# Key pages and probabilities turned by VectorE in 32x32 blocks, values four pages at a time, weight splits on GpSimd

## What is computed

```
h = rmsnorm(x);  q,k,v,g_a,u,v_s,g_b,m_a,m_b = split(h @ w_in)        # 1024 x 5632
prompt:  causal attention over its own 512 keys (8 heads of 64), bias by distance
sample b: 16 cache pages of 128 tokens (table page_table[b]); blocks of 256 tokens
   gate  = q . mean(k of block);  keep the 3 best of 8 blocks per head and query
   s     = q . k + bias;  softmax over the kept pages and the new tokens;  out = p @ v
y_a = attn * silu(g_a);   y_b = gelu(u) * (tril(w_s) @ layernorm(gelu(v_s)) + b_s) * silu(g_b)
y   = rmsnorm(x + (sigmoid(m_a) * (y_a @ w_pa) + sigmoid(m_b) * (y_b @ w_pb)) @ w_o)
```

## Time and profile before

| | us |
|---|---|
| median of three runs | 585.2 |
| the profiled execution, its own time | 585.09 |
| its span, first to last instruction | 583.3 |

### The profile page before, as it was taken

The page is one execution under the profiler, slowest core; times in us unless marked ns, Lnnn a source line. Parts: engine busy times, 40 slices in busy tenths (PEclk is TensorE's granted clock), DMA queues, the critical chain, the costliest instruction groups (busy, mean ns, idle before and its releaser), DMA issues.

```text
span 583.3 us, 14963 instructions
## 1 busy us (share of the span) xinstructions
PE 571.0 (98%) x6072; PEld 524.7 (90%) x6072; DVE 315.3 (54%) x749; ACT 211.9 (36%) x461; POOL 24.3 (4%) x39
## 2 busy tenths in 40 slices
PE   8999999999999999999999999999999999999994
PEld 6999999998899899999889998999999999998763
DVE  5622324345456555666756666786463255695514
ACT  5523222334333434543454451241153241234313
POOL 2101111000000000000000000010000000000002
PEclk9999999999999999999999999999999999999998
DMA  8447334755586766767576577885879857152003
GB/s 263 133 164 236 112 111 129 213 187 179 168 256 182 235 189 206 223 195 243 173 234 210 183 253 248 281 251 169 259 236 338 286 179 257 57 190 88 1 8 145
DMA packets 73421, 111.89 MB, mean 192 GB/s; under 512 B 5485, under 2 KB 35194, under 8 KB 73354
## 3 DMA queue, kind: packets, MB, share of 16 engines
q1 hardware_dynamic: 71978, 107.33, 57.5%
q0 software_dynamic: 1232, 3.36, 2.0%
q10 hardware_dynamic: 144, 0.26, 0.1%
HBM read 106.39 MB, written 4.53 MB: 190 GB/s over the span
## 4 chain that ended last, share of the span: by engine, by line
PE 95%; DVE 2%; issue 1%; ACT 1%; POOL 0%; POOLq 0%; DVEq 0%; ACTq 0%
PE BK L497 43%; PE BK L643 9%; PE BK L517 8%; PE BK L848 7%; PE BK L655 6%; PE BK L669 5%; PE BK L579 2%; PE BK L720 2%; PE BK L727 2%; PE BK L531 2%; PE BK L737 2%; PE BK L773 1%; PE BK L695 1%; PE BK L868 1%; PE BK L564 1%
## 5 line engine op out<-in xcount | busy, mean ns | idle before, releaser
L497 PE MATMUL BK<-XH,WH 128*128 128x272 f32 x672 | 212.4, 316 | 0.0
L497 PE MATMUL BK<-XH,WL 128*128 128x272 f32 x672 | 194.3, 289 | 0.0
L497 PE MATMUL BK<-XL,WH 128*128 128x272 f32 x672 | 193.2, 288 | 0.0
L497 PEld LDWEIGHTS BK<-XH,WH 128*128 128x128 f32 x672 | 126.7, 189 | 9.9 <-issue 8.7
L497 PEld LDWEIGHTS BK<-XL,WH 128*128 128x128 f32 x672 | 127.2, 189 | 0.0
L497 PEld LDWEIGHTS BK<-XH,WL 128*128 128x128 f32 x672 | 126.5, 188 | 0.0
L1141 DVE TENSOR_TENSOR WL<-WRAW,WH 128x1024 fp32r<-128x1024 f32 x51 | 62.2, 1220 | 37.5 <-ACT WH L897 37.3
L643 PE MATMUL BK<-CST,KRAW 128*128 128x128 f32 x512 | 77.2, 273 | 0.8 <-DVE ATS L1330 0.5
L643 PEld LDWEIGHTS BK<-CST,KRAW 128*128 128x128 f32 x512 | 60.7, 141 | 2.5 <-issue 2.3
L1239 DVE COPY KT<-BK 128x512 f32<-128x512 f32 x64 | 44.0, 687 | 32.8 <-PE BK L643 32.7
L897 ACT ACTIVATE WH<-WRAW 128x1024 fp32r<-128x1024 f32 x52 | 54.8, 1055 | 18.6 <-PE BK L517 18.6
(11 more groups left out here) (205 smaller groups left out, 803.4 us busy)
## 6 DMA issues: line engine op xcount, KB each, us to landing
KRAW<-in_cache_k SPq DMA_DIRECT2D x128, 256.0 KB, 3.5
VRAW<-in_cache_v SPq DMA_DIRECT2D x120, 256.0 KB, 3.8
WRAW<-in_w_in SPq DMA_DIRECT2D x21, 1024.0 KB, 6.0
WO<-in_w_o SPq DMA_DIRECT2D x4, 1024.0 KB, 7.8
XR<-in_x_prompt SPq DMA_DIRECT2D x4, 512.0 KB, 5.6
VEX<-in_cache_v SPq DMA_DIRECT2D x8, 256.0 KB, 4.9
WRAW<-in_w_pb SPq DMA_DIRECT2D x4, 512.0 KB, 6.4
WRAW<-in_w_pa SPq DMA_DIRECT2D x4, 512.0 KB, 5.9
```

What stands on the lines that cost most here:

```text
L497: last = mm(BK[h][:, 0:HALF], w[:, n % 2, k, :], x[:, k, cols], start=(i == 0 and w is WH and x is XA), stop=(i == KC - 1 and w is WL))
```

## The change

1. **Pages.** VectorE turns a page in 32x32 blocks straight from `KRAW` to `KT` (`page_turn`), all 128 pages, once the page's loads have landed. TensorE's transposes and both copies go. As a block turn doesn't cross groups of 32 partitions, the page is laid out for it by its load: four DMAs, one for each 128 columns, to 32 partitions each, in pieces of 512 bytes. Queries (`QC`) and the new keys (`KSS`) are laid out in the same way.
2. **Probabilities** are turned by VectorE as well (`probs_turn`), into `PT` and `PLT`.
3. **Values** are loaded by groups of four pages, each page on 32 partitions with four tokens in each, by one DMA a page; six places for groups, and a schedule of their own (`PLACE`, `load_step`). Their steps start at lag 24 instead of 20.
4. **Two score banks** (banks 4 and 2) alternate between samples. The steps of the samples' chain are set by functions (`gate_step` to `out_step_of`), and bank 3 serves all small results.
5. **Prompt** attention has 12 blocks instead of 16 (the two short ones are joined), in steps 5 to 68. ScalarE copies both heads' turned probabilities, and scales the samples' outputs.
6. **GpSimd** makes the low parts of 31 weight tiles, the gate products and the low part `YBL`.

```diff
-LAG = 20
+LAG = 24
+CLOSE = {27: 130, 28: 134, 29: 135, 30: 136, 31: 137}
+PLACE = [0 if q % 2 == 0 and q <= 24 or q == 28 else 1 if q <= 9 else 2 if q <= 23 else 3 + (q - 25) % 4 for q in range(32)]
+BLOCKS = [(c, ys) for c in range(PAIRS) for ys in ((0, 1), (2,), (3,))]
+def block_at(t):
+    if t % 16 in (5, 10, 15) and 5 <= t < 16 * PAIRS:
+        return 3 * (t // 16) + t % 16 // 5 - 1
+def load_step(q):
+    first = {1: 8, 11: 64, 25: 113, 26: 115, 27: 117}
+    return first[q] if q in first else values_step(value_place(q)[2])
 # SyncE
             def load_k(i):
-                wait(sp, kt_pe, i - KR + 1)
+                wait(sp, kt_ok, i - KR + 1)
                 page = sp.snap(k_regs[i % 4], min_val=0, max_val=cache_k.shape[1] - 1)
-                sp.dma_start(KRAW[:, i % KR, :], cache_k[0, bass.ds(page, 1)].rearrange("a p h d -> (a p) (h d)")).then_inc(k_ld[i % KR], 16)
+                rows = cache_k[0, bass.ds(page, 1)].rearrange("a (t p) h d -> (a t) p (h d)", p=4)
+                for a in range(4):
+                    sp.dma_start(KRAW[32 * a:32 * a + 32, i % KR].rearrange("t (p n) -> t p n", p=4), rows[:, :, a * P:(a + 1) * P]).then_inc(k_ld[i % KR], 16)
+            def load_v(q):
+                place, _, prior = value_place(q)
+                sp.load(v_regs, PTB[0:1, 4 * q:4 * q + 4])
                 if prior is not None:
                     sp.wait_ge(pv_pe, prior + 1)
+                for j in range(4):
+                    page = sp.snap(v_regs[j], min_val=0, max_val=cache_v.shape[1] - 1)
+                    sp.dma_start(VP[place][32 * j:32 * j + 32], cache_v[0, bass.ds(page, 1)].rearrange("a (t p) h d -> (a t) p (h d)", p=4)
+                                 ).then_inc(v_ld[place], 16)
 # TensorE
-            def turn_page(i):
-                for c in range(PAIRS):
-                    last = pe.transpose(BK[2 + i % 2][:, c * P:(c + 1) * P], KRAW[:, i % KR, c * P:(c + 1) * P], IDN)
             def page_scores(q):
-                pe.wait_ge(kt_act, 2 * q + 2)
-                pe.wait_ge(kt_dve, 2 * q + 2)
+                pe.wait_ge(kt_ok, 4 * q + 4)
                 if x == 0:
-                    wait(pe, ex_ok, 5 * b)
+                    wait(pe, ex_ok, 5 * (b - 1))
-            def turn_probs(b, t):
-                for x in range(4):
-                    pe.wait_ge(ex_ok, 5 * b + x + 1)
-                    last = pe.transpose(bk[:, x * P:(x + 1) * P], SC[:, x * P:(x + 1) * P], IDN)
 # ScalarE
-            def page_out(i):
-                copy(KT[:, i % KB], BK[2][:].rearrange("p (c n) -> p c n", c=PAIRS)).then_inc(kt_act, 1)
-            def probs_out(b):
-                copy(PT[:], BK[2][:].rearrange("p (x n) -> p x n", x=4)).then_inc(pt_ev, 1)
+            def scale_out(b):
+                act.activation(OTS[:], OUT[:, 0:P], ACT.Copy, scale=RL[:, 0:1]).then_inc(ots_ok, 1)
 # VectorE
-            def page_out(i):
-                dve.tensor_copy(KT[:, i % KB], BK[3][:].rearrange("p (c n) -> p c n", c=PAIRS)).then_inc(kt_dve, 1)
+            def page_turn(i):
+                dve.wait_ge(k_ld[i % KR], 64 * (i // KR + 1))
+                wait(dve, sc_pe, (i - KB) // 4 + 1)
+                dve.transpose(KT[:, i % KB].rearrange("q s (p t) -> q p s t", p=4),
+                              KRAW[:, i % KR].rearrange("q (p s d) -> q p s d", p=4, s=4)).then_inc(kt_ok, 1)
+            def probs_turn(b):
+                    dve.transpose(PT[:].rearrange("p x n -> p (x n)"), SC[:]).then_inc(pt_ok, 1)
+                dve.transpose(PLT[0:32, :], SCL[:]).then_inc(pl_ok, 1)
                 if t % 4 == 0 and 4 <= t <= 128:
-                    split_lo(n + 1)
 # GpSimd
+            def split_lo(n):
+                pool.wait_ge(w_hi, n + 1)
+                pool.tensor_tensor(WL[:, n % 2], WRAW[:, n // 2 % 2, :, n % 2 * P:(n % 2 + 1) * P], f32(WH[:, n % 2]), ALU.subtract).then_inc(w_lo, 1)
+            for t in range(4, 129):
+                if t % 4 == 0:
+                    split_lo(N_QKV + t // 4 + 1)
+                if t % 4 == 1 and 85 <= t < 101:
+                    gate_product((t - 85) // 4)
+                if t == 117:
+                    pool.wait_ge(ybh_ok, 1)
+                    pool.tensor_tensor(YBL[:], G[:, GB:GB + 4, :], f32(YBH[:]), ALU.subtract).then_inc(ybl_ok, 1)
```

## The result

The changed kernel takes **708.7 us** (median of four runs, 706.9 to 710.6) against 585.3 (584.5 to 585.7) for the kernel before on the same chip: a ratio of 1.211, 95% interval 1.208 to 1.213. The forecast was 558 us, range 524 to 598, so both the sign and the size are wrong. The profiled execution has a span of 707.0 us.

What follows compares the result with a forecast made beforehand. The prediction took TensorE's instruction stream as the bound: 585 us less 64 taken off it gives 521, plus 32 for SyncE's queue becoming late gives 553; it took 558 us, range 524 to 598.

Steps and rivals of the forecast that it cites:

- What bounds before: Kernel before the change: bound by TensorE's instruction stream, busy 98% of the 583.3 us span at full clock.
- what TensorE gives up: TensorE in the steps: page transposes 58 us, probability transposes 3.6, the rest about 2.5; 64 us in all, leaving 521.
- VectorE and GpSimd: Page turn on VectorE taken at 0.69 us, weight split on GpSimd at 2.37 us; neither expected to bind.
- SyncE's queue: the part that decides: SyncE's DMA issues go from 128 + 128 to 512 + 128, making the queue late by 32 us.
- A page on the queue, 1.93 us: SyncE's time per K page: arithmetic once, table load share, four times MOVE and issue; bounds 1.70 to 2.19 us.
- the second stretch: Steps 68 to 128: SyncE's queue needs 163.1 us against TensorE's 133, adding 30 us.
- Rival 3: SyncE's page issues cost 0.616 us each, 2.55 a page: slower than before, 622 us, range 586 to 622, chance 0.18.
- Rival 2: TensorE stays the bound as SyncE's issues following each other cost less: 521 to 535 us, chance 0.22.
- rival 4: DMA engines bind, pages at double cost or worse: +40 us on steps 68 to 128, about 575, chance 0.04.
- rival 5: VectorE's page turn costs 1.22 us or GpSimd's split is late: about 575 us, chance 0.04.
- A quarter more for the pages: DMA engines, steps 84 to 128: pages in 512-byte pieces cost a quarter more, 105 us of work in a 120 us stretch.
- Full if these gaps are short: TensorE's clock: stays full if its gaps ahead of the score matmuls, waiting for page turns, are short.

Runs made afterwards that it cites:

- e5: The changed kernel with each K page and each V page loaded whole by one DMA to 128 partitions: 526.1 us, ratio 0.899.
- e9: The changed kernel with only the token order changed, a partition's four tokens lying 32 apart instead of consecutive: 601.1 us, ratio 1.029.
- e1: The changed kernel with each K page loaded by one whole DMA of 2 KB rows to 128 partitions: 569.6 us, ratio 0.976.
- e10: The changed kernel with K page DMAs split over SyncE's and ScalarE's queues, tokens 32 apart, whole V pages, probabilities turned on TensorE: 553.3 us, ratio 0.943.
- e3: The kernel before with each K page load cut into four DMAs of 32 partitions with whole 2 KB rows: 601.4 us.
- e13: The changed kernel with tokens 32 apart, and SyncE reading the page number anew before three of each K page's four DMAs: 701.9 us, ratio 1.199.
- e2: The changed kernel with each K page's 512-byte pieces loaded by one DMA with a four-dimensional source: 822.1 us, ratio 1.403.
- e6: The changed kernel with whole K pages, and V pages on 32 partitions in 2 KB rows instead of 8 KB runs: 570.4 us, ratio 0.973.

## Why the prediction was wrong

- **What bounds before; what TensorE gives up: right.** 64 us were to leave the stream, for a floor of 521; e5 measured 526.1, with TensorE at 97% and a full clock.
- **VectorE and GpSimd: right.** 0.71 us for the turn (bounds 0.48 to 1.22) and 2.38 for the split. In e5, where nothing else is late, TensorE waits 2.2 us in all for page turns and never for a split of GpSimd.
- **Which engine decides: right.** "SyncE's queue: the part that decides" is what the chain shows.
- **A page on the queue, 1.93 us: the step that failed.** It took 0.333 us an issue from the earlier trace rows, where 115 of the 128 issues have that price within 1 ns, but for another form: 128 partitions with one row each. No row had the new one. The new form cost 0.564 at the median and 0.597 on average. The bounds, 1.70 to 2.19, varied only how many MOVEs and how much arithmetic are repeated; the issue's own price, the largest term, had no bound at all in this sum. With the measured 3.15 us a page, and 0.09 for its share of the table load, the prediction's own sum gives 176 us for steps 24 to 68 (44 x 3.24 + 30.8 + 2.9; +59 over TensorE), 235 for the second stretch (+102) and some 81 for the first 24 steps (24 x 3.24 and the weight loads) against 57 (+24): 706 us. The first 24 steps had no term for the queue at all. That the sum comes within 3 us of 708.7 is in part luck, as the values' and weights' terms in it are still the forecast's.
- **The count of instructions lay within its bounds, not at its likeliest.** The sum took the arithmetic once a page, and the trace has it for each issue (128 times at L476 and 384 at L480). With the cheap order a page measured 2.03 us at the median, 2.12 with its share of the table load, against 1.93 taken and 2.19 as the bound. Long issues add 0.22 on average, more than the 0.09 allowed, and from 200 us on the DMA share is 0.92 and over. With 2.34 us a page the prediction's sum gives some 596 (+20, +53 and +2 in the three stretches), and e9 took 601.
- **Could a row have given the price?** The kernel before has one load in pieces of 512 B taken out of order, the mixing weights, cited for its landing time only the earlier trace rows. Its issue is 47% over that of the earlier trace rows:

```profile
L453 SPq DMA_DIRECT2D WSR<-in_w_s x1: 488/488/488, 345.2 to 345.2; - x1
```

  But it proves nothing of the order: the plain loads on either side of it took 0.738 and 1.983 us, and the same load took 0.427 in the changed kernel and in e9, no more than the plain load of `LNB` in the trace before (0.433). What the earlier trace rows did show is that the price goes by form (0.426 for a weight load); the size for a K page in pieces had to be measured.
- **The rivals.** Rival 3 had the mechanism and the sign, and it decided as it said, from 0.54 per issue. Its price, 0.616 for an issue with all around it, came from bursts of value issues, again in the plain form; the measured distance is 3.15 / 4 = 0.79. Its 622 us and chance of 0.18 were too low for the same reason as the forecast. (Redone, its second stretch is 197 us and +64, which its 622 rests on, and not 200 and +67.) Rival 2 (the queue keeps waiting for buffers) fell with L476's single wait, rival 4 with pages that land in 2.7 us at the median, and rival 5 with the prices of the turn and the split.
- **DMA engines: hidden, and under-priced.** A quarter more for the pages was taken. That the values' destination of 32 partitions costs too was missed: 43 us between e1 and e5. In the changed kernel it is hidden, as the queue stands in front (share 0.67 over the steps); whole V pages gave 4 us on one queue even at the cheap issue. In e1 the engines are the bound from 300 us on (share 0.99 to 440 us), and in e10 their share is 1.11 from 300 to 400. The Trainium skill's rule that spoke against the split (DMA: Bandwidth & Descriptors, section "Rules for kernel authors": no split over disjoint partitions) was worth its place: e3, the plain split with nothing else, cost 16 us, though with the queue's slack used up and the engines' share hardly changed (0.71 against 0.67 from 200 to 300 us). Its rate for 64 KB, 138 GB/s (section "Bandwidth"), is not what bound: the average over the kernel was 158 GB/s with idle engines, and e10 moves 260 in its busiest stretch.
- **TensorE's clock.** "Full if these gaps are short": they weren't. In the changed kernel 24 stretches, 153 us in all, were granted 1.2 GHz instead of 2.4, each but the last behind a pause of TensorE of 2 us or more; in e9 11 stretches with 72 us, in e5 only one at the very end. e13, with the changed kernel's queue time, has 24 stretches with 161 us. So the clock goes with the gaps; what it adds to them wasn't measured by itself.

## What to carry to other kernels

Price a DMA issue by its form, not by its queue: a form that the trace doesn't show needs its own wide bounds, and if it is multiplied by 500 it is measured first, together with the number of DMA engines that it is spread over. When a change takes work off the bound engine and pays with issues, count the queue's time per step as carefully as TensorE's, since a queue that waits 170 us for buffers hides one issue a page and not four. And when the bound is a queue, ask first for another queue or another order of the source, before taking the rest of the change back: here this turned 709 us into 553.

## What the runs showed of the hardware that was not expected

- The issue of a DMA of [4 pieces of 512 B] x 32 partitions took 0.564 us with four consecutive tokens in a partition and 0.317 with tokens 32 apart: same bytes, same destination. One row of 2 KB in each of 32 partitions: 0.316. No run shows why the order counts. Loads behind a page take longer too: weight loads of one form took 0.582 us at the median in the changed kernel and 0.425 in e9.
- All four in one DMA with a four-dimensional source: 0.61 us for the issue behind another kind of load, 3.0 right behind a page, as only four DMA engines move it. For that one the Trainium skill (DMA: Bandwidth & Descriptors, section "Why a DMA increments its semaphore by 16 and not by 1") says that the engines that take part are the largest number up to 16 that divides the slowest dimension of both sides, which is 4 here. The trace agrees: four landings for each page in e2, 16 for each DMA in the changed kernel.
- A V page on 32 partitions with four tokens in each costs the DMA engines more than one on 128: 2 KB packets averaged 132 ns with half of them of that kind (e6), 98 with none (e5).
